# Token-major gate and up chunks in the convolutional feed-forward of a four-layer kernel

## The reference

```python
def causal_dwconv(u, w, b):          # w: (3, C), one filter per channel, over tokens
    y = lax.conv_general_dilated(u, w[:, None, :], window_strides=(1,),
                                 padding=[(CONV_WIDTH - 1, 0)], ..., feature_group_count=C)
    return y + b

def conv_ffn(h, w_up, conv_w, conv_b, w_down):
    u = causal_dwconv(h @ w_up, conv_w, conv_b)
    g, up = jnp.split(u, 2, axis=-1)
    return (jax.nn.silu(g) * up) @ w_down
...
        x = x + conv_ffn(rms_norm(x, ln_ffn_g[i]), w_up[i], conv_w[i], conv_b[i], w_down[i])
```

## Time and profile before

| | |
|---|---|
| median of 3 runs | 1863.47 us |
| profiled execution: its time, its span | 1863.22 us, 1861.4 us |
| PE busy, share of the span | 1850.0 us, 99% |
| PE weight loads | 1565.7 us, 84% |
| DVE busy | 1238.5 us, 67% |
| ACT busy | 1061.4 us, 57% |
| POOL busy | 95.6 us, 5% |
| granted TensorE clock | 1.0 (2.4 GHz) |
| DMA | 361.89 MB, mean 194 GB/s |

### The profile page before, as it was taken

The page is one execution under the profiler, slowest core; times in us unless marked ns, Lnnn a source line. Parts: engine busy times, 40 slices in busy tenths (PEclk is TensorE's granted clock), DMA queues, the critical chain, the costliest instruction groups (busy, mean ns, idle before and its releaser), DMA issues. The chain is left out here.

```text
span 1861.4 us, 24532 instructions
## 1 busy us (share of the span) xinstructions
PE 1850.0 (99%) x9552; PEld 1565.7 (84%) x9552; DVE 1238.5 (67%) x1807; ACT 1061.4 (57%) x1536; POOL 95.6 (5%) x163
## 2 busy tenths in 40 slices
PE   8999999999999999999999999999999999999999
PEld 7889998879999888888888888888888888888887
DVE  6868777677777755557876654665555788665555
ACT  6756555666555643468855544363535886546352
POOL 2000000000000001000010010101010001000100
PEclk9999999999999999999999999999999999999999
DMA  8445564537556567644555466676675446456664
GB/s 265 156 140 200 172 207 165 174 114 230 184 182 204 184 201 251 210 172 159 179 195 204 161 223 227 218 260 215 212 234 196 159 158 230 152 190 209 219 234 136
DMA packets 164493, 361.89 MB, mean 194 GB/s; under 512 B 7782, under 2 KB 20683, under 8 KB 163867
## 3 DMA queue, kind: packets, MB, share of 16 engines
q1 hardware_dynamic: 154400, 327.24, 51.8%
q0 software_dynamic: 9520, 32.89, 6.0%
q10 hardware_dynamic: 459, 0.20, 0.0%
HBM read 348.73 MB, written 11.58 MB: 194 GB/s over the span
## 5 line engine op out<-in xcount | busy, mean ns | idle before, releaser
L1335 ACT ACTIVATE w_hi<-raw 128x1024 fp32r<-128x1024 f32 x620 | 633.3, 1054 | 451.1 <-PE bank L515 192.6
L2089 DVE TENSOR_TENSOR w_lo<-raw,w_hi 128x1024 fp32r<-128x1024 f32 x620 | 733.9, 1223 | 196.1 <-ACT w_hi L1335 189.2
L513 PE MATMUL bank<-w_hi,r_hi 128*128 128x512 f32 x1344 | 531.3, 395 | 1.2 <-DVE r_lo L2113 0.6
L515 PE MATMUL bank<-w_hi,r_lo 128*128 128x512 f32 x1344 | 523.9, 390 | 0.0
L514 PE MATMUL bank<-w_lo,r_hi 128*128 128x512 f32 x1344 | 523.2, 389 | 0.0
L513 PEld LDWEIGHTS bank<-w_hi,r_hi 128*128 128x128 f32 x1344 | 252.4, 188 | 56.4 <-DVE r_lo L2113 2.4
L515 PEld LDWEIGHTS bank<-w_hi,r_lo 128*128 128x128 f32 x1344 | 252.3, 188 | 53.5
L514 PEld LDWEIGHTS bank<-w_lo,r_hi 128*128 128x128 f32 x1344 | 252.6, 188 | 50.0
L513 PE MATMUL bank<-w_hi,z_hi 128*128 128x512 f32 x656 | 258.9, 395 | 1.5 <-DVE z_lo L2089 0.7
L515 PE MATMUL bank<-w_hi,z_lo 128*128 128x512 f32 x656 | 255.7, 390 | 0.0
L514 PE MATMUL bank<-w_lo,z_hi 128*128 128x512 f32 x656 | 255.6, 390 | 0.0
(11 more groups left out here) (231 smaller groups left out, 1557.4 us busy)
## 6 DMA issues: line engine op xcount, KB each, us to landing
raw<-in_w_in SPq DMA_DIRECT2D x79, 1024.0 KB, 5.1
raw<-in_ffn_w_down SPq DMA_DIRECT2D x44, 1024.0 KB, 7.9
raw<-in_w_up SPq DMA_DIRECT2D x40, 1024.0 KB, 5.2
raw<-in_ffn_w_gate SPq DMA_DIRECT2D x40, 1024.0 KB, 5.6
raw<-in_ffn_w_up SPq DMA_DIRECT2D x40, 1024.0 KB, 8.1
raw<-in_w_down SPq DMA_DIRECT2D x22, 1024.0 KB, 4.8
raw<-in_w_out SPq DMA_DIRECT2D x16, 1024.0 KB, 5.1
by_block<-qk POOLq DMA_DIRECT2D x20, 512.0 KB, 3.3
```

The lines of the kernel that those rows point to most:

```text
L513: pe.matmul(out_, lh, rh, start=start, stop=False, skip_group_check=True)
L515: return pe.matmul(out_, ll, rh, start=False, stop=stop, skip_group_check=True)
L1335: A_(w_hi[:, n % NH, :], raw[:, u % NS, HALF * h:HALF * (h + 1)], ACT.Copy).then_inc(hi_ready, 1)
L2089: return V.tensor_tensor(dst, src, hi.bitcast(F32), ALU.subtract)
```

## The change

In steps 0 to 3 the gate and up chunks are computed token-major by `quarter`; steps 4 and 5 stay as they are. For each of these eight chunks of a layer, ScalarE copies the two banks, times the norm's factor, to `gu` in `v` (`gu_stage`), VectorE turns the blocks (`gu_turn`), POOL carries them over DRAM (`tokens_moved`), and ScalarE puts them in order into the tile that `main` and `taps` read (`unfold`). `scale` is gone for these steps. `gu`, `gu_blocks` and `gu_moved` are single buffers; `by_token` is double. The order of the units becomes gate 0, up 0, gate 1, up 1, gate 2, down 0, up 2, gate 3, down 1, up 3, gate 4, down 2, up 4, down 3, gate 5, down 4, down 5, on all engines and in the loads.

```diff
+def conv_units(j):
+    return ((0, 2, None), (4, 6, 10), (8, 12, 16), (14, 18, 22), (20, 24, 26), (28, 28, 30))[j]
...
+        gu = v_flat[:, 0:1024].rearrange("p (t c) -> p t c", t=TB)
+        gu_blocks, gu_moved = v_flat[:, 1024:2048], qk_flat[:, 3072:4096]
...
+            def tokens_moved(f):
+                for j in range(4):
+                    for up in range(2):
+                        n = gu_at(f, j, up)
+                        pool.wait_ge(gu_turned, 2 * n + 2)
+                        pool.dma_start(by_token[n % 2], gu_blocks).then_inc(gu_out, 16)
+                        pool.wait_ge(gu_out, 16 * (n + 1))
+                        if n:
+                            pool.wait_ge(unfolded, 2 * n)
+                        for a in range(4):
+                            pool.dma_start(gu_moved[32 * a:32 * a + 32, :].rearrange("c (b r) -> c b r", b=4),
+                                           by_token[n % 2].rearrange("(b c) (a r) -> a c b r", b=4, a=4)[a]
+                                           ).then_inc(gu_in, 16)
...
                 def chunk_part(j, up, i):
                     def free(b):
-                        if j:
-                            pe.wait_ge(scaled, 22 * f + 4 * (j - 1) + 2 * up + b + 1)
-                    quarter_rows(u0 + ffn_units(j)[up] + i // 2, i // 2, i % 2, (A, B)[up],
-                                 None if j or up else KT * norm_at(where, n), free)
+                        if 0 < j < 5:
+                            pe.wait_ge(gu_staged, 2 * gu_at(f, j - 1, up) + b + 1)
+                        if j == 5:
+                            pe.wait_ge(scaled, scaled_at(f, 4, up) + b + 1)
+                    (quarter if j < 4 else quarter_rows)(
+                        u0 + conv_units(j)[up] + i // 2, i // 2, i % 2, (A, B)[up],
+                        *((r_hi, r_lo) if j < 4 else ()), None if j or up else KT * norm_at(where, n), free)
...
+                def gu_stage(j, up, t):
+                    chunk_wait(u0 + conv_units(j)[up] + 1, h0 + 2 * j + up, t)
+                    if j == 0:
+                        act.wait_ge(rstd_ready, norm_at(where, n) + 1)
+                    if gu_at(f, j, up):
+                        act.wait_ge(gu_turned, 2 * gu_at(f, j, up))
+                    A_(gu[:, t, :], bank[(A, B)[up] + t][:, :], ACT.Identity, scale=rstd[:, t:t + 1]
+                       ).then_inc(gu_staged, 1)
+
+                def unfold(j, up, b):
+                    act.wait_ge(gu_in, 64 * (gu_at(f, j, up) + 1))
+                    if j:
+                        act.wait_ge(conv_done, 22 * f + 4 * (j - 1) + 2 * up + b + 1)
+                    A_(stage[:, 1024 * up + 512 * b:1024 * up + 512 * b + 512].rearrange("p (k b q) -> p k b q", b=4, q=32),
+                       gu_moved.rearrange("p (b k q) -> p k b q", b=4, q=32)[:, 4 * b:4 * b + 4, :, :],
+                       ACT.Copy).then_inc(unfolded, 1)
...
+                def gu_turn(j, up, t):
+                    at = gu_at(f, j, up)
+                    dve.wait_ge(gu_staged, 2 * at + t + 1)
+                    if at:
+                        dve.wait_ge(gu_out, 16 * at)
+                    V.transpose(gu_blocks.rearrange("p (a m t q) -> p t a m q", a=4, t=TB, q=32)[:, t, :, :, :],
+                                gu[:, t, :].rearrange("p (m a q) -> p a m q", a=4, q=32)).then_inc(gu_turned, 1)
```

More of the change, by code:

```diff
@@ L1512, in ffn_conv @@
                 hi(u0 + 5, 1)
+                gu_stage(0, 1, 0)
+                gu_stage(0, 1, 1)
+                hi(u0 + 6, 0)
+                unfold(0, 0, 0)
+                unfold(0, 0, 1)
+                hi(u0 + 6, 1)
+                main(0, 0, 0)
+                main(0, 0, 1)
+                hi(u0 + 7, 0)
                 silu(0, 0)
+                hi(u0 + 7, 1)
+                gu_stage(1, 0, 0)
                 silu(0, 1)
[L1517 removed]
+                gu_stage(1, 0, 1)
@@ L1538, in ffn_conv @@
[L1538 to L1562, removed]
+                hi(u0 + 11, 0)
@@ new lines, in ffn_conv @@
+                silu(1, 0)
+                hi(u0 + 11, 1)
+                gu_stage(2, 0, 0)
+                silu(1, 1)
+                gu_stage(2, 0, 1)
+                hi(u0 + 12, 0)
+                unfold(1, 1, 0)
+                unfold(1, 1, 1)
+                hi(u0 + 12, 1)
+                main(1, 1, 0)
+                main(1, 1, 1)
+                hi(u0 + 13, 0)
+                hi(u0 + 13, 1)
+                hi(u0 + 14, 0)
+                prod_hi(1, 0)
+                unfold(2, 0, 0)
@@ new lines, in ffn_conv @@
+                prod_hi(1, 1)
+                unfold(2, 0, 1)
+                hi(u0 + 14, 1)
+                main(2, 0, 0)
+                main(2, 0, 1)
+                hi(u0 + 15, 0)
+                silu(2, 0)
+                hi(u0 + 15, 1)
+                gu_stage(2, 1, 0)
+                silu(2, 1)
+                gu_stage(2, 1, 1)
+                hi(u0 + 16, 0)
+                hi(u0 + 16, 1)
+                hi(u0 + 17, 0)
+                hi(u0 + 17, 1)
+                gu_stage(3, 0, 0)
@@ new lines, in ffn_conv @@
+                gu_stage(3, 0, 1)
+                hi(u0 + 18, 0)
+                unfold(2, 1, 0)
+                unfold(2, 1, 1)
+                hi(u0 + 18, 1)
+                main(2, 1, 0)
+                main(2, 1, 1)
+                hi(u0 + 19, 0)
+                hi(u0 + 19, 1)
+                hi(u0 + 20, 0)
+                prod_hi(2, 0)
+                unfold(3, 0, 0)
+                prod_hi(2, 1)
+                unfold(3, 0, 1)
+                hi(u0 + 20, 1)
+                main(3, 0, 0)
@@ new lines, in ffn_conv @@
+                main(3, 0, 1)
+                hi(u0 + 21, 0)
+                silu(3, 0)
+                hi(u0 + 21, 1)
+                gu_stage(3, 1, 0)
+                silu(3, 1)
+                gu_stage(3, 1, 1)
+                hi(u0 + 22, 0)
+                hi(u0 + 22, 1)
+                hi(u0 + 23, 0)
+                hi(u0 + 23, 1)
+                hi(u0 + 24, 0)
+                unfold(3, 1, 0)
+                unfold(3, 1, 1)
+                hi(u0 + 24, 1)
+                main(3, 1, 0)
@@ new lines, in ffn_conv @@
+                main(3, 1, 1)
+                hi(u0 + 25, 0)
+                hi(u0 + 25, 1)
+                hi(u0 + 26, 0)
+                prod_hi(3, 0)
+                prod_hi(3, 1)
+                main(4, 0, 0)
+                hi(u0 + 26, 1)
+                main(4, 0, 1)
+                hi(u0 + 27, 0)
+                silu(4, 0)
+                silu(4, 1)
+                hi(u0 + 27, 1)
+                hi(u0 + 28, 0)
+                main(4, 1, 0)
+                main(4, 1, 1)
+                hi(u0 + 28, 1)
@@ L2368, in ffn_conv @@
[L2368 to L2394, removed]
-                    product(j, 0)
-                    product(j, 1)
+                lo(u0 + 14, 0)
```

226 lines of the change are left out of this document (175 added, 51 removed).

## The result

The changed kernel takes 1888.01 us (median of 4 runs, 1886.57 to 1890.35) against 1863.78 before: a ratio of 1.0129, 95% interval 1.0117 to 1.0141. It is 24 us slower, where 1870 was forecast, 7 us slower, with a range up to 1884. The direction was right; the loss is more than three times the forecast one. The profiled execution has a span of 1888.5 us, 27.1 more than before.

A forecast was written before the change was run, and what follows sets the result against it. TensorE's own matmuls were taken to bound the kernel; 1863.2 - 10.2 saved + 0.3 for gaps + 2 x 8.5 of stalls from moves over DRAM = 1870.3, said as 1870, with 8 in 10 between 1857 and 1884.

The forecast's parts named there:

- TensorE's saving, 10.2 us: Feed-forward gate and up chunks: eight token-major chunks in each of two layers, 0.64 us less each, 10.2 us in all.
- The doubt of 0.3 a step at the switch: PE where up ends and down begins: possible gap of 0.3 us per changed step; 0.3 in all taken, range 0 to 2.6.
- The list of costs beside it: Added ScalarE stages and unfolds, VectorE turns, POOL DMAs: ScalarE near 23 of 32.6 us, DMA engines 79%; none the bound.
- The chain of moves as what decides: Moves of 13.1 us in in-order queues stall TensorE 8.5 us a layer; case 1867.2 to 1885, chance 0.45.
- the walk: Step-by-step timing of layer 0's feed-forward queues from its first matmul, giving 8.5 us of TensorE stall a layer.
- The signs named beforehand: PE's waits for w_lo: first at unit 13 of each layer, most at unit 15, some 8 us a layer.
- from the end of the second turn ... to the first read's issue ... I take 3.9: The write in each move over DRAM: 3.84 us in the second block, taken as 3.9.
- The clock, left at 1.00: TensorE's granted clock in both feed-forwards: assumed to stay at 1.00, the 2.4 GHz level.
- The cover: Rival: moves stay hidden, TensorE stalls under 3.3 us a layer; 1853 up to 1859.6, chance 0.29.
- Congestion of the weights: Rival: DMA engines congest, w_up loads land over 11 us after their slot is free; 1892, chance 0.06.
- The Trainium skill's fit for one DMA: 2.0 us + bytes / 436 GB/s: 2.3 us per 128 KB read, reading 4 us, and no stall left.
- 1 us more on each read costs 12 in all: Six reads a layer hang on the chain of moves, so each extra 1 us per read adds 12 us in all.

The follow-up runs named there:

- the better order: Changed kernel, steps 0 to 3: unfold behind the four halves due, stage and turn ahead of silu and second taps; 1854.18 us against 1864.17, ratio 0.9948.
- the run with traffic alone: Kernel before with the moves' DMAs added (a write and four reads per chunk) and nobody waiting for them; 1864.13 us against 1864.16, ratio 1.0003.

## Why the prediction was right in kind and wrong in size

- **TensorE's saving, 10.2 us: right.** Pitch 0.2267 in every undisturbed changed chunk. With the way over DRAM left out the whole gain is 9.0, with the better order 10.0. The doubt of 0.3 a step at the switch came to nothing. Not foreseen: TensorE waits for r_lo at the start of each changed layer, 0.6 at a time.
- **The list of costs beside it, hidden: right**, shown by the run without the way over DRAM and, for the DMA engines, by the run with traffic alone.
- **The chain of moves as what decides: right in mechanism.** PE stalls for the second units of chunks, as the walk had it: by 2.9 at unit 13, 1.0 at 15, 2.8 at 19 and 2.8 at 25 of layer 0 (1.75, 3.4, 1.8 and 1.1 in the walk), and first by 1.2 at unit 7, where the walk named no stall (its 28.9 + 9.1 = 38.0 stands against 33.6 + 5.44 = 39.0). The signs named beforehand, first at unit 13 and most at unit 15, were misses. Gate 2 is staged 9.3 us late, not 7.6. The walk had the unfolds at 28.9, 52.5, 77.3, 102.1 and 137.3 after the start of layer 0; measured from 125.64 they are at 32.1, 56.9, 80.8, 107.2 and 144.4.
- **The step that failed is the write: "from the end of the second turn ... to the first read's issue ... I take 3.9".** The row came from the second block, where SP's next load is issued after the write (at 670.17 for the one of 669.33) and none is under way; all 20 writes there are so, and take 2.9 to 3.9. Here a write is issued with one or two loads under way and takes 4.8 to 8.7. On the five moves of layer 0's chain, writes took 7.25, 5.38, 5.35, 5.60 and 5.66 from issue to first read against 3.6: 11.2 us more. The reads gave back about 5 of it, mostly 6.6 to 8.9 where 9.2 was taken, and the first turn was 0.9 late: net 7, and the last unfold of the chain is 7.1 late. The layer's feed-forward, to its last transposes, took 198.6 us where the walk had 191.3 and before had 187.8. I had bounded the reads from 20 moves and the write from rows of one kind; the upper bound was missing, and so was the question what is under way at the write's issue, though the earlier trace rows show that a 1 MB load can take 9.9 us in company.
- **The clock, left at 1.00 without a reason, was the second term**: layer 1 took 202.5 us, 3.9 more than layer 0, and its two stretches at 1.2 GHz account for that: six wide matmuls at 0.43 and 27 narrow at 0.21 in place of 0.227 and 0.12 make 3.7. Together 7.3 + 7.3 + 3.9 are 18.5 of the 20 us by which the profiled span missed the sum; the rest lies outside these stages and was not traced.
- **Rivals.** The cover does hold at another place in the list; as the lists were written it didn't. Congestion of the weights is out: the traffic alone costs nothing, and in layer 0 of the changed kernel the loads of w_up land in 6.9 us (median), not over 11. The Trainium skill's fit for one DMA ("DMA: Bandwidth & Descriptors", Anatomy of one DMA) gives 3.2 us for 512 KB; the runs agree where little is in flight, 2.9 to 3.7, and differ by a factor near two among weight loads, with medians of 5.7 and 6.1. The measurement decides. What the page says on shared engines (Issuing engines are not separate DMA queues) agrees with SP's write of 6.3, which SP's own queue could explain as well.
- **Length and place both count.** That 1 us more on each read costs 12 in all was right as a proportion for the lists as written: 7 us more on the chain gave 7 us more of stall a layer. But it holds for that order alone, which the forecast left as given. With the old order, shorter moves end the stalls (1855.13 without the moves, 1856.20 without the write); with moves as long as before, another order does (1855.14 and 1854.18). A move of 15 us stalls TensorE when weights due in 5 us stand behind it.

What stays open: how much of each write's length is the wait of its packets and how much their slower flow, whether SP's write shares engines or a queue with the loads, and why four waits of 2.8 us and more left the clock alone while two did not.

## What to carry to other kernels

A long-latency wait in an in-order list costs what stands behind it, not its own length: put work with near deadlines ahead of it, and let the wait sit where only its own consumers follow. Take a DMA's duration from rows where as much is under way at its issue as there will be; a duration from an idle queue is a lower bound. When the order of a kernel with short stalls is changed, look at TensorE's clock before the time is read: the same waits can cost more or less by it. A faster TensorE stage is worth its saving only after the engines that feed it have been checked at the new pace.

## What the runs showed of the hardware

- Three waits of TensorE of 2.8 to 2.9 us in layer 0 and one of 3.4 in layer 1 left the granted clock at 1.00; two of 2.8 and 2.9 in layer 1 were followed by some 3 and 6 us at the 1.2 GHz level. With stage and turn ahead, waits of 1.92 and 2.16 us were followed by such a stretch and one of 1.96 was not. The length of the wait alone does not tell them apart.
- A 512 KB write from SBUF to DRAM took 2.9 to 3.9 us where no load was under way at its issue, even with 1 MB loads issued 0.8 to 3.1 us later (20 writes of the second block and five with unfold moved; four more of these took 2.9 to 3.9 beside one load issued 6.6 us or more before). In layer 0 of the changed kernel it took 5.1 to 5.4 where one load had been issued 1.5 us before, 6.0 and 6.9 where it was 2.7 and 3.0 us before, and 7.0 and 8.0 with two under way. With half-sized loads it took 3.7 in the median, and 6.3 when SP issued it.
